# Mixture-of-experts weights: one ScalarE operation per load, and TensorE's products in two groups

## The reference, cut to what matters

```python
def _swiglu(x, w_gate, w_up, w_down):
    return (jax.nn.silu(x @ w_gate) * (x @ w_up)) @ w_down

def _moe_swiglu(x, w_router, b_router, w_gate, w_up, w_down):   # two of eight experts per token
    ...
    for e in range(N_EXPERTS):                  # w_gate[e], w_up[e]: 1024 x 3584, w_down[e]: 3584 x 1024
        out = out + combine[..., e:e + 1].astype(x.dtype) * _swiglu(x, w_gate[e], w_up[e], w_down[e])
    return out
```

## Time and profile before

| | |
|---|---|
| median of three runs | 2880.84 us |
| the profiled execution: span | 2871.6 us |
| TensorE matmul busy | 2536.3 us (88%) |
| TensorE weight load busy | 1996.6 us (70%) |
| VectorE busy | 2080.5 us (72%) |
| ScalarE busy | 1536.3 us (53%) |
| bytes by DMA | 598.07 MB, mean 208 GB/s |
| chain that ended last, by engine | PE 62%, DVE 26%, ACT 8%, issue 2%, ACTq 1% |

### The profile page before, as it was taken

The page is one execution under the profiler, slowest core; times in us unless marked ns, Lnnn a source line. Parts: engine busy times, 40 slices in busy tenths (PEclk is TensorE's granted clock), DMA queues, the critical chain, the costliest instruction groups (busy, mean ns, idle before and its releaser), DMA issues.

```text
span 2871.6 us, 31529 instructions
## 1 busy us (share of the span) xinstructions
PE 2536.3 (88%) x11727; PEld 1996.6 (70%) x11727; DVE 2080.5 (72%) x2254; ACT 1536.3 (53%) x1876; POOL 18.1 (1%) x29
## 2 busy tenths in 40 slices
PE   7987799978876999999999999978777998787898
PEld 3736677767455878888888888757556886556787
DVE  6587787665775898989889898976755554665554
ACT  1221443433144888788888888854534444444443
POOL 0000000000100000000000000000000000000000
PEclk8997899987887999999999999989687998877899
DMA  8450357742243999999999999966031554203352
GB/s 265 151 180 30 103 178 278 263 165 91 67 139 114 362 352 341 357 353 349 349 348 368 348 357 356 344 223 200 0 112 64 177 190 143 87 30 103 118 189 88
DMA packets 274341, 598.07 MB, mean 208 GB/s; under 512 B 28722, under 2 KB 35200, under 8 KB 273026
## 3 DMA queue, kind: packets, MB, share of 16 engines
q1 hardware_dynamic: 252144, 580.30, 57.4%
q10 hardware_dynamic: 22034, 15.67, 2.0%
HBM read 594.87 MB, written 1.06 MB: 208 GB/s over the span
## 4 chain that ended last, share of the span: by engine, by line
PE 62%; DVE 26%; ACT 8%; issue 2%; ACTq 1%; DMA 0%; DVEq 0%; POOLq 0%
PE PS L211 60%; DVE WL L167 7%; DVE MW L167 4%; ACT WH L203 3%; PE PS L219 3%; DVE AR L167 2%; DVE WF L167 1%; ACTq L146 1%; ACT AR L203 1%; DVE MOD L167 1%; DVE HF L167 1%; ACT WF L203 1%; DVE ATR L167 1%; DVE HTR L167 1%; ACT L203 1%
## 5 line engine op out<-in xcount | busy, mean ns | idle before, releaser
L167 DVE TENSOR_TENSOR WL<-RG,WH 128x1024 fp32r<-128x1024 f32 (+1 forms) x558 | 919.2, 1647 | 405.7 <-ACT WH L203 378.0
L203 ACT ACTIVATE WH<-RG 128x1024 fp32r<-128x1024 f32 x782 | 827.5, 1058 | 592.6 <-PE PS L211 542.7
L211 PE MATMUL PS<-WH,HTR 128*128 128x512 f32 (+3 forms) x2920 | 919.2, 391 | 58.3 <-DVE HTR L167 31.4
L211 PEld LDWEIGHTS PS<-WH,HTR 128*128 128x128 f32 x2920 | 558.4, 194 | 180.7 <-DVE HTR L167 34.2
L211 PE MATMUL PS<-WL,HTR 128*128 128x512 f32 (+3 forms) x1460 | 569.3, 390 | 0.0
L211 PE MATMUL PS<-WH,ATR 128*128 128x512 f32 x1624 | 519.5, 393 | 17.1 <-DVE WL L167 9.1
L211 PEld LDWEIGHTS PS<-WH,ATR 128*128 128x128 f32 x1624 | 307.1, 189 | 82.6 <-DVE WL L167 15.7
L211 PE MATMUL PS<-MW,HTR 128*128 128x512 f32 x1332 | 329.6, 396 | 7.1 <-DVE MW L167 6.5
L211 PEld LDWEIGHTS PS<-WL,HTR 128*128 128x128 f32 x1460 | 283.2, 194 | 53.4
L211 PE MATMUL PS<-WL,ATR 128*128 128x512 f32 x812 | 317.9, 391 | 0.0
L211 PEld LDWEIGHTS PS<-MW,HTR 128*128 128x128 f32 x1332 | 244.3, 188 | 66.3 <-DVE MW L167 17.8
(11 more groups left out here) (226 smaller groups left out, 1980.4 us busy)
## 6 DMA issues: line engine op xcount, KB each, us to landing
RG<-in_moe_w_gate SPq DMA_DIRECT2D x112, 1024.0 KB, 6.0
RG<-in_moe_w_up SPq DMA_DIRECT2D x112, 1024.0 KB, 6.3
RG<-in_moe_w_down SPq DMA_DIRECT2D x112, 1024.0 KB, 6.4
RG<-in_w_ff SPq DMA_DIRECT2D x64, 1024.0 KB, 5.2
RG<-in_mod_w SPq DMA_DIRECT2D x48, 1024.0 KB, 5.2
RG<-in_w_in SPq DMA_DIRECT2D x36, 1024.0 KB, 5.3
RG<-in_w_out SPq DMA_DIRECT2D x16, 1024.0 KB, 5.1
RG<-in_ffn_w_gate SPq DMA_DIRECT2D x14, 1024.0 KB, 5.2
```

Of the source, the lines that this page charges most:

```text
L167: return self.did(lambda: self.e.tensor_tensor(o, a, b, op))
L203: return self.did(lambda: self.e.activation(o, a, f, bias=bias, scale=scale))
L211: return self.did(lambda: self.e.matmul(o, l, r, start=start, stop=stop))
```

## The change

The high half of a pair is made by one ScalarE operation of 2048 columns, issued where the first part's stood; the second part's is left out. It waits until both parts of the buffer have been used. A count `his` per part numbers the high halves as `los` numbers the low ones. On TensorE, per load, the eight products with the high half of the weights come first, behind a wait for the high half; then a wait for the low half, and the four products with it. `used` is counted twice per load as before, but both times among the last four products. In `down`, the products alternate between the two PSUM banks. `down_last`, VectorE's program and the order of the loads stay.

```diff
@@ class Weights: plan
                     if k == 0:
                         self.lows += 1
+                        self.highs += 1
                         p.both = flat[:, 0:2 * CV], hi, lo
+                    else:
+                        self.parts[i - 1].pair = p
                 else:
                     self.lows += 1
-                p.los = self.lows
+                    self.highs += 1
+                p.los, p.his = self.lows, self.highs
@@ his
         for p in self.parts[self.next_hi:self.next_hi + n]:
-            if p.prev is not None:
-                a.wait_ge(self.used, p.prev + 1)
+            if p.i and p.his == self.parts[p.i - 1].his:
+                continue
+            for q in (p, p.pair):
+                if q is not None and q.prev is not None:
+                    a.wait_ge(self.used, q.prev + 1)
             a.wait_ge(self.landed[p.load.slot], p.load.use)
-            a.act(p.hi, p.src, ACT.Copy).then_inc(self.hi)
+            if p.both is not None:
+                a.act(p.both[1], p.both[0], ACT.Copy).then_inc(self.hi)
+            else:
+                a.act(p.hi, p.src, ACT.Copy).then_inc(self.hi)
@@ los
             if p.both is not None:
-                v.wait_ge(self.hi, p.i + 2)
+                v.wait_ge(self.hi, p.his)
                 v.tt(p.both[2], p.both[0], p.both[1].bitcast(F32), SUB).then_inc(self.lo)
             elif p.i == 0 or p.los != self.parts[p.i - 1].los:
-                v.wait_ge(self.hi, p.i + 1)
+                v.wait_ge(self.hi, p.his)
@@ pe_moe
             def up(parts, b, u):
-                for p in parts:
-                    pe.wait_ge(P.lo, p.los)
-                    for k in range(p.kk):
-                        kk = p.k0 + k
-                        x = pe.mm3(PS[:, b, :], HE[0][:, u, kk, :], HE[1][:, u, kk, :], p.h3[:, k, :], p.l3[:, k, :], kk == 0,
-                                   kk == 7)
-                    x.then_inc(P.used)
+                for pair in zip(parts[::2], parts[1::2]):
+                    pe.wait_ge(P.hi, pair[0].his)
+                    for p in pair:
+                        for k in range(p.kk):
+                            kk = p.k0 + k
+                            for z in range(2):
+                                pe.mm(PS[:, b, :], HE[z][:, u, kk, :], p.h3[:, k, :], kk == 0 and z == 0, False)
+                    pe.wait_ge(P.lo, pair[0].los)
+                    for p in pair:
+                        for k in range(p.kk):
+                            kk = p.k0 + k
+                            x = pe.mm(PS[:, b, :], HE[0][:, u, kk, :], p.l3[:, k, :], False, kk == 7)
+                        x.then_inc(P.used)
@@ down
-                for p in P.of["moe_down", e, n]:
-                    pe.wait_ge(P.lo, p.los)
+                parts = P.of["moe_down", e, n]
+                cs = [slice(h * 512, (h + 1) * 512) for h in range(2)]
+                for pair in zip(parts[::2], parts[1::2]):
+                    pe.wait_ge(P.hi, pair[0].his)
                     pe.wait_ge(s_v, j, "at")
...
-                        x = pe.mm3(PS[:, h, :], EAT[0][:, j % 2, i, :], EAT[1][:, j % 2, i, :], p.h3[:, 0, c], p.l3[:, 0, c],
-                                   n == 0 and i == 0, n == 6 and i == 3)
-                    x.then_inc(P.used)
+                    for p in pair:
+                        i = p.k0
+                        for z in range(2):
+                            for h in range(2):
+                                pe.mm(PS[:, h, :], EAT[z][:, j % 2, i, :], p.h3[:, 0, cs[h]], n == 0 and i == 0 and z == 0, False)
+                    pe.wait_ge(P.lo, pair[0].los)
+                    for p in pair:
+                        i = p.k0
+                        for h in range(2):
+                            x = pe.mm(PS[:, h, :], EAT[0][:, j % 2, i, :], p.l3[:, 0, cs[h]], False, n == 6 and i == 3)
+                        x.then_inc(P.used)
```

More of the change, by code:

```diff
@@ L234, in __init__ @@
         self.i, self.load, self.src, self.hi, self.lo, self.kk, self.k0, self.last = i, load, src, hi, lo, kk, k0, last
-        self.prev, self.both, self.los = None, None, 0
+        self.prev, self.both, self.los, self.his, self.pair = None, None, 0, 0, None
 class Weights:
@@ L243, in __init__ @@
         self.RG, self.pairs = RG, pairs
-        self.at, self.user, self.lows = 0, {}, 0
+        self.at, self.user, self.lows, self.highs = 0, {}, 0, 0
         self.landed = [signal(f"{name}landed{s}", by=16) for s in range(RING)]
@@ L2052, in down @@
                             pe.wait_ge(s_v, e - 1, f"de{h}")
-                    i = p.k0
-                    for h in range(2):
-                        c = slice(h * 512, (h + 1) * 512)
-                        x = pe.mm3(PS[:, h, :], EAT[0][:, j % 2, i, :], EAT[1][:, j % 2, i, :], p.h3[:, 0, c], p.l3[:, 0, c],
-                                   n == 0 and i == 0, n == 6 and i == 3)
-                    x.then_inc(P.used)
+                    for p in pair:
[9 more added lines that the diff above has]
+                        x.then_inc(P.used)
             for g in range(2):
```

## The result

The kernel after takes 2864.88 us (median of four runs, 2863.31 to 2867.94) where the kernel before took 2881.8 us beside it (four runs, 2880.45 to 2883.02). The ratio is 0.9948, with a 95% interval of 0.9933 to 0.9962: faster by 11 to 19 us. A ratio in this document stands with the 95% interval behind it.

What follows compares the result with a forecast made beforehand. TensorE was taken to set the pace, its idle time being winnable: (14.3 - 1.2) x 0.8 = 10.5, plus 1.7 and 0.3, made 12.5 us. Span 2871.6 less 12.5, plus 9.2, gave 2868.3 us; own range 2864 to 2872, overall 2861 to 2882.

Steps and rivals of the forecast that it cites:

- High products first: TensorE in the experts' stage: low half needed 1.8 us later, winning 2.0 of 2.4 us per expert, 10.5 us in all.
- One copy: ScalarE's 2048-column copy: 1.92 us; pair ready 0.3 us earlier where ScalarE is behind, 0.86 later where it waits for TensorE.
- More waits: On TensorE, 334 loads get an added wait: cost taken as 0, bounds 0 and 0.11 us each.
- Transfers: Weight loads in the experts' stage: asked rate rises from 353 to 358 GB/s, at no cost.
- The rival by which the time could not fall below 2868 us: Experts' stage: HBM peak of 358 GB/s lets the window shrink by 12.6 us at most; chance 0.05.
- The start: First loads of the experts' stage: TensorE's idle wait for a low half at 918.72 us goes, 1.7 us won.
- The end: Last expert, bound by VectorE: only 0.3 us won; its 1.2 us share of the stalls drops out.
- All stalls go: Experts' stage: all TensorE stalls and part of its short matmul waits vanish, some 20 us, giving 2861 us; chance 0.12.
- VectorE holds: Each expert: VectorE's three waits grow by 2.6 us, so only 0.7 us per expert is won, giving 2875 us; chance 0.17.
- Slower by ScalarE's hold: Tight stretch of each expert: five later copies delay VectorE, 1.0 us lost per expert, giving 2887 us; chance 0.10.
- Slower by added waits: TensorE: added waits break the weight loads' run-ahead, costing 37 us, giving 2905 us; chance 0.03.
- does nothing: TensorE's waits merely move to the products with the low half, giving 2881 us; chance 0.05.

Runs made afterwards that it cites:

- the copy alone: Kernel before with only the single ScalarE copy of 2048 columns, TensorE's program unchanged: ratio 1.0017 (1.0007 to 1.0026).
- the order alone: Kernel after with ScalarE making each high half in two copies of 1024 columns, as before; ratio to the kernel before 0.9952 (0.9937 to 0.9968).
- the kernel without the fold: Kernel after with VectorE's four 128x1024 operations (4.9 us) left out of the last expert: 2864.05 us, ratio to the kernel before 0.9942.
- four first: Kernel after with only four high products ahead of the wait for the low half, per part four high then two low: ratio to the kernel before 0.9987.

## Why the prediction was right

The time forecast was 2868.3 us and the measured one 2864.9, inside the forecast's own range of 2864 to 2872; the side, and the forecast's own case among the rivals, came true: the stage became 12.5 us shorter, the sum of the prediction to a tenth. That exactness is luck: two other profiles of the same kernel give 12.1 and 13.7 us, and the terms err both ways.

- *High products first: right, and a little low.* Expected was that four of an expert's six waits go, that the fifth is just covered, and that of the sixth some 0.4 us stays. The kernel after has the fifth at 0.21 and the sixth at 0.52 us, 0.39 us of cost after the 0.17 each. An expert won 2.36 us (126.16 - 123.80) where 2.0 were expected, and the six middle pieces 13.1 us, more than the whole term of 10.5. The rest of an expert, 0.36, is within what the matmul waits of the earlier trace rows hold, 5.8 us over seven experts, which the sum left to a rival; they are gone in the kernel after, but that they make up the 0.36 is not shown.
- *One copy: right.* 1.92 us was taken, 1920 ns measured. The line through 633 ns at 512 columns and 1062 at 1024 held to 2048. That the copy's lateness of 0.86 us has a price and that the new slack covers it are both shown, by the copy alone (-2.9 us) and by the order alone (0.8 us from the kernel after).
- *More waits: right.* Taken at 0, measured 0 with 1000 of them.
- *Transfers: right that they cost nothing, wrong about how near their limit is.* The rate is 359 GB/s in the stretch where 358 was expected. ScalarE's waits for data grew, 9.5 us on WH and 2.0 on MW where the earlier trace rows had 1.7 on MW; in the kernel's last profile they are 2.5 us on WH, with experts of the same length. The rival by which the time could not fall below 2868 us is out: with a third of TensorE's work gone the rate was 368 GB/s over 700 us. That speaks against 358 GB/s as a ceiling of a core that runs alone (the Trainium skill, Perfetto Trace Analysis, Engine Utilization); the same section's remark on a lone core agrees.
- *The start: sized too high.* 1.7 us were expected. TensorE did start its high products at 921.22 us, 0.37 us after VectorE began that load's low half at 920.85, instead of idling. But the piece up to the first gathering gave 1.1 us in all: ahead of those products TensorE still idled 0.84 us, and it waited 0.33 us for the low half behind them, at 923.20.
- *The end: the sign was wrong.* "The last expert gives only the 0.3 us of VectorE's advance." The bound was named rightly (shown by the kernel without the fold), and VectorE's last low half even came 1.2 us sooner after the gathering. The step that failed is that the longer wait of TensorE was taken to cost nothing beyond what it gave back: it grew from 1.67 to 3.40 us, and the granted clock fell behind it, 1.6 us that no term held. The branch took another 1.3 us; it varies by 1.6 us within one kernel, so this is no finding about the change. Together the last expert lost 1.7 us.

So 14.2 us up to the last gathering, where 10.5 + 1.7 = 12.2 were expected, and -1.7 instead of +0.3 from there: the two errors of 2 us cancel.

**Of what was to be seen**, these came: copies at 1.92 us, 38 waits to 11 and all in the group's middle, the DMA rate, and no wait for a high half. TensorE reached `down_last` 17 us sooner in the stage (983.3 instead of 1000.4 us from its start), not 12. One reading was wrong: VectorE's waits in blocks 3 and 4 were to be longer each. The longest is (1.72 us), but in all they are fewer and shorter, 30.7 us in 48 against 48.3 in 65: VectorE has the same work in 12.5 us less.

**The base of the sum.** The 9.2 us between the profiled span and the median were said to lie around the span. In every other profiled run of this study only 1.8 us do. By that the profiled execution before took some 2873.4 us, an estimate, less than any of the four timed (2880.45 or more); its experts start at 902.7 us, earlier than in all other profiles. It did the forecast no harm, since it stood on both sides.

**The rivals.** *All stalls go* (20 us) was nearest of them: up to the last gathering 14.2 of its 16 us came. *VectorE holds* is out: it had VectorE's three waits at 1286, 1297 and 1305 us grow by 2.6 us in all, and from 1256 to 1347 us none is left; an expert won 2.2 us in the mean, not 0.7. *Slower by ScalarE's hold*: the copy alone is that mechanism without the slack, and it cost 2.9 us, not 6. *Slower by added waits* and *does nothing* are out.

## What to carry to other kernels

Where an engine waits many times for short stretches on the second of two inputs, let it do first what needs only the first input. How much that gives can be read from the waits one by one: add up what each would advance it, and stop where the supplier has no pause left. Do the same at the last, odd piece of the loop too: there the supplier's backlog falls due in one wait, and behind one of 3.4 us TensorE also ran at a lower clock for a while. Cut up at an operation that comes once an expert, the middle of a stage repeats to 0.1 us from profile to profile of one kernel (one piece of the kernel after: 123.80, 123.83 and 123.84 us), where the whole kernel's median tells of some 6 us.

## What the runs showed of the hardware

- TensorE's granted clock stayed at 1.00 after idle times of 0.51, 0.69, 1.67 and, in the copy alone, 2.29 us. It fell after 2.30 us (0.66 in the five microseconds around the restart, in the kernel without the fold), 2.51 us (0.66, four first) and 3.40 us (0.89, then 0.76). Twelve matmuls took 2.8 us at 1.00, 4.4 us in these three kernels and 5.25 us in the order alone, after 3.39 us.
- GpSimd's operations on 128x1024 fp32 slow VectorE's subtraction on 128x2048: up to 4.31 us instead of 2.29. Moving 4.9 us of work from VectorE to GpSimd cost VectorE 7.8 us.
- At the branch behind `down_last` VectorE is idle for 6.7 to 6.8 us, in every kernel, and TensorE for 4.8 to 6.4 us in three profiles of the same kernel.
- 1000 fulfilled semaphore waits on TensorE cost nothing that can be measured (0.9990 to 1.0007).
- One core took weights from HBM at 368 GB/s for 700 us, at a DMA share of 1.00.
